# Two units' low halves taken by DMA at other places, one more unit split, and the order of a few steps around it

## The chip, the cores and the metric

The kernel runs on one core of a Trainium2 chip. The metric is the device time of one execution in microseconds (us); lower is better. The engines are named as the profile names them: PE (TensorE matmul), PEld (its weight loads), DVE (VectorE), ACT (ScalarE), POOL (GpSimd) and SP (SyncE), each with its own instruction queue; they meet only at semaphores.

## The reference

Two decoder layers on a tensor x of 256 tokens by 1024 channels, all in float32:

```python
def pool_conv_layer(x, ...):
    h = rms_norm(x, norm_g)
    a, bv, bg, z = split(h @ w_in)              # 1024 | 1024 | 1024 | 2048 columns
    ya = pool_w(trailing_mean(a) - a) * pool_scale      # windows of 2, 4, 8, 16 tokens
    u = causal_depthwise_conv(bv * sigmoid(bg), 31 taps) + conv_b
    yb = silu(layer_norm(u))
    return (concat(ya, yb) * silu(z)) @ w_out

def moba_layer(x, ...):
    q, k, v, z = split(rms_norm(x) @ w_in)      # 16 heads of 64
    q, k = per_head_rms_norm(q) * 64 ** -0.5, per_head_rms_norm(k)
    o = causal_softmax(q k^T - slope * distance) v
    return (o * silu(z)) @ w_out

x = x + pool_conv_layer(x); x = x + moba_layer(x)
```

With 256 tokens and attention blocks of 256 the second layer is plain causal attention over all tokens.

## The kernel before, in words

**Units.** All weights are cut into 49 units of 1 MB (128 partitions by 2048 floats), numbered in the order in which PE uses them: 0 to 7 gate and value of the convolution in turn (`BG`, `BV`), 8 to 11 the pooled channels (`A`), 12 to 15 the gates of the convolution half (`ZB`), 16 the pooling maps (`PW`), 17 to 20 the gates of the pooled half (`ZA`), 21 to 28 the output projection (`OA`, `OB`), 29 to 48 the second layer. SP loads unit n into place n % 4 of `raw`, once the last reader of unit n - 4 is through (L397).

**Native and split units.** A unit in `NATIVE` is multiplied as it is, in float32. Of any other, ACT writes a rounded copy `w_hi` in two halves of 1024 columns (`cut_hi`, L459), DVE writes `w_lo` = raw - `w_hi` (`cut_lo`, L723), and PE makes three products for each tile (`product`, L1058 to L1060). For the four units in `ADDED`, DVE has no part in this: ACT writes also -`w_hi` into `w_lo` (L462), and a DMA from POOL's queue adds raw to it (`added_low`, L424); PE waits for its landing. `cut_slot` says in which of four places of `w_hi` and `w_lo` a unit lies; ahead of unit 29 three of them rotate and the fourth holds unit 22 and then the convolution's result `yb`.

**The convolution.** In the loop over n = 1 to 21 (n names the unit that PE works on) ACT and DVE also make the 31 taps of eight channel tiles, two tiles a pair. `conv_plan` writes the order out before: with running sums of the free time of DVE and ACT in each unit (`slot_work` says what else they do there) it takes for each tap either a product by ACT (two multiplications, L542) that DVE adds (L845), or two fused multiply-adds on DVE (L841, called singles below). What is left at n = 21 goes to DVE as singles. Twelve products for each of two pairs are added by DMA instead: ACT multiplies (L518), POOL issues the adding DMA (L433), both by `side_items`. `window_sums` (L812 to L824) makes the pooling means of units 8 to 11 from `AP`, into which ACT copies a PSUM bank (L568) as soon as DVE is through with the copy before it.

**From the last tap to the output projection.** DVE adds the eight tiles to one (`fold_mean`, L858). PE takes the mean over channels by a matmul (`channel_mean`, L1181), DVE subtracts it (`centre`, L865), ACT squares (L467), DVE adds (L752), PE sums (L1135). `MEAN_AT` and `SUM2_AT` say behind which output product of units 21 to 24 PE makes these two matmuls: unit index in `OA`, row tile 0 or 1, column tile 0 to 7. Then come the root, `normalise`, the silu and `yb`, and behind them in the queues of ACT and DVE the cuts of units 26 to 28, which PE needs for `closing`.

**The second layer.** Units 33 to 44 run in three pairs for each octet of heads (keys, queries, values), 16 steps a pair, with scores, transposes and values of the octet before put between the steps. Keys and queries pass through PSUM bank `TR` for their transposes (L1251), and ACT copies them out (`qk_turn_out`, L680); the transposes of the probabilities (L1285) use the same bank. `KT_AT` gives the steps of the two key transposes, 28 and 32. `qk_squares` (L670) squares the banks of a pair, token tile by token tile.

## Time and profile before

| | |
|---|---|
| median of 3 runs | 332.69 us (332.54 to 332.81) |
| the profiled execution | 333.14 us |
| its span in the trace | 331.3 us |
| PE busy | 325.0 us (98%), 2212 matmuls |
| DVE busy | 256.2 us (77%) |
| ACT busy | 230.4 us (70%) |
| chain that ended last | PE 93%, DMA 3%, ACT 1%, DVE 1%, issue 1% |
| PE's clock | 0.9 or more of full speed in all 40 slices of the span, which is the level of 2.4 GHz |

An engine is read as waiting where a row carries "idle before", with what released it. The chain is followed back from the last instruction; a piece of it that isn't PE stands where PE waited, or just made it. A DMA issue on POOL is short, and its transfer lands long after; the time from issue to landing stands in an extra line of an answer on a tile or line. 331.3 us of span and 333.14 us of device time differ by 1.8 us that lie around the span.

### The profile page before, as it was taken

To read this page: it belongs to the slowest core of one execution; us is meant where nothing else is said; L and a number is where in the kernel's file an instruction comes from. 1 tells how busy PE (TensorE), PEld (TensorE's weight loads), DVE (VectorE), ACT (ScalarE), POOL (GpSimd) and SP (SyncE) were. 2 spreads that over 40 slices of the span, in tenths; PEclk is the share of its full clock that TensorE was granted. 3 is DMA by queue.
4 is the path that set the end of the run, shared out by engine and by line. 5 is a ranking of instruction groups with operands and counts; after the bars stand their busy time and mean duration, and the time that the engine had idled before them with its cause. 6 is when DMAs were issued, how large, how long until landed. Compare 5 with 4: busy or idle time off the path is not lost.

```text
span 331.3 us, 5760 instructions
## 1 busy us (share of the span) xinstructions
PE 325.0 (98%) x2212; PEld 296.2 (89%) x2212; DVE 256.2 (77%) x475; ACT 230.4 (70%) x429; POOL 51.8 (16%) x58
## 2 busy tenths in 40 slices
PE   8999999999999999999999999999999999999995
PEld 8899999999989999997999999988887776778885
DVE  2699989999689999996886898747556877748633
ACT  4677999994999897935775557824756666575630
POOL 0050024424422310120000000005500231400000
PEclk9999999999999999999999999999999999999999
DMA  7979488979999998676629343780634323200003
GB/s 277 409 272 357 146 267 217 202 164 349 276 252 345 167 380 296 130 174 208 254 103 403 130 133 133 279 347 10 245 127 166 135 99 132 108 0 2 2 0 127
DMA packets 12842, 64.77 MB, mean 195 GB/s; under 512 B 1424, under 2 KB 1552, under 8 KB 6544
## 3 DMA queue, kind: packets, MB, share of 16 engines
q1 hardware_dynamic: 8064, 53.78, 43.2%
q0 software_dynamic: 4608, 10.49, 17.3%
q8 instruction: 17, 0.28, 0.3%
q10 hardware_dynamic: 144, 0.15, 0.2%
q14 instruction: 9, 0.07, 0.1%
HBM read 52.88 MB, written 1.05 MB: 163 GB/s over the span
## 4 chain that ended last, share of the span: by engine, by line
PE 93%; DMA 3%; ACT 1%; DVE 1%; issue 1%; POOL 0%; ACTq 0%; POOLq 0%
PE bank L1058 25%; PE bank L1060 23%; PE bank L1059 23%; PE bank L1118 5%; PE bank L1092 4%; DMA w_lo<-raw 3%; PE bank L1166 2%; PE bank L1272 2%; PE bank L1299 2%; PE bank L1135 2%; PE bank L1126 2%; PE bank L1285 2%; PE bank L1251 1%; ACT scratch L467 1%; DVE scratch L752 1%
## 5 line engine op out<-in xcount | busy, mean ns | idle before, releaser
L723 DVE TENSOR_TENSOR w_lo<-raw,w_hi 128x1024 fp32r<-128x1024 f32 x76 | 90.3, 1222 | 19.6 <-ACT w_hi L459 19.4
L1058 PE MATMUL bank<-h_hi,w_hi 128*128 128x256 f32 x304 | 86.6, 285 | 0.4 <-DMA w_lo<-raw 0.4
L459 ACT CAST w_hi<-raw 128x1024 fp32r<-128x1024 f32 x84 | 84.4, 1048 | 2.7 <-PE bank L1060 2.7
L1060 PE MATMUL bank<-h_hi,w_lo 128*128 128x256 f32 x304 | 86.0, 283 | 0.0
L1059 PE MATMUL bank<-h_lo,w_hi 128*128 128x256 f32 x304 | 86.0, 283 | 0.0
L1058 PEld LDWEIGHTS bank<-h_hi,w_hi 128*128 128x128 f32 x304 | 58.3, 192 | 0.9 <-issue 0.8
L1059 PEld LDWEIGHTS bank<-h_lo,w_hi 128*128 128x128 f32 x304 | 58.3, 192 | 0.1
L1060 PEld LDWEIGHTS bank<-h_hi,w_lo 128*128 128x128 f32 x304 | 58.3, 192 | 0.0
L841 DVE SCALAR_TENSOR_TENSOR scratch<-scratch,params 128x256 f32<-128x256 f32 x108 | 44.1, 484 | 0.2
L1058 PE MATMUL bank<-w_hi,h_hi 128*128 128x512 f32 x96 | 39.2, 408 | 0.0
L1058 PE MATMUL bank<-ya_hi,w_hi 128*128 128x256 f32 x128 | 38.1, 297 | 0.0
L1060 PE MATMUL bank<-w_hi,h_lo 128*128 128x512 f32 x96 | 37.6, 391 | 0.0
L1059 PE MATMUL bank<-w_lo,h_hi 128*128 128x512 f32 x96 | 37.5, 391 | 0.0
L1060 PE MATMUL bank<-ya_hi,w_lo 128*128 128x256 f32 x128 | 36.1, 282 | 0.0
L1059 PE MATMUL bank<-ya_lo,w_hi 128*128 128x256 f32 x128 | 36.1, 282 | 0.0
L433 POOL DMA_DIRECT2D side_v<-side_ring x24 | 21.1, 908 | 70.8 <-ACT side_ring L518 65.7
L542 ACT ACTIVATE scratch<-scratch,params 128x256 f32<-128x256 f32 x76 | 31.9, 505 | 0.0
L845 DVE TENSOR_TENSOR scratch<-scratch 128x512 f32<-128x512 f32 x38 | 25.7, 692 | 1.4 <-ACT scratch L542 0.2
L1058 PEld LDWEIGHTS bank<-ya_hi,w_hi 128*128 128x128 f32 x128 | 24.4, 191 | 2.0 <-issue 1.7
L1059 PEld LDWEIGHTS bank<-ya_lo,w_hi 128*128 128x128 f32 x128 | 24.5, 191 | 0.1
L1060 PEld LDWEIGHTS bank<-ya_hi,w_lo 128*128 128x128 f32 x128 | 24.4, 191 | 0.0
L444 POOL TENSOR_SCALAR scratch<-scratch 128x8 f32<-128x8 f32 x8 | 4.3, 535 | 122.1 <-DVE scratch L1018 121.9
(106 smaller groups left out, 549.0 us busy)
## 6 DMA issues: line engine op xcount, KB each, us to landing
raw<-w SPq DMA_DIRECT2D x49, 1024.0 KB, 6.3
side_v<-side_ring POOLq DMA_DIRECT2D x24, 256.0 KB, 8.2
w_lo<-raw POOLq DMA_DIRECT2D x8, 512.0 KB, 8.1
X<-xT SPq DMA_DIRECT2D x2, 512.0 KB, 5.2
out<-X SPq DMA_DIRECT2D x4, 256.0 KB, 2.6
consts<-const SPq DMA_DIRECT2D x1, 290.0 KB, 13.5
params<-vec ACTq DMA_DIRECT2D x1, 149.0 KB, 4.9
```

The costliest lines, as they stand in the source:

```text
L433: pool.dma_start(side_v[:, pair, item % 2, :, :], side_home(pair, item), accum_op=ALU.add).then_inc(side_added[pair][item % 2], 16)
L459: nc.scalar.copy(halves(w_hi, cut_slot(n), half), halves(raw, n % RAW, half)).then_inc(hi_cut, 1)
L542: last = nc.scalar.mul(product_home(product)[:, i, :], U[:, c, k:k + S], column(CW + TAPS * c + k))
L723: nc.vector.tensor_tensor(halves(w_lo, cut_slot(n), half), halves(raw, n % RAW, half), halves(w_hi, cut_slot(n), half).bitcast(F32), ALU.s ...
L841: nc.vector.scalar_tensor_tensor(V[:, c, :], U[:, c, k:k + S], column(CW + TAPS * c + k), V[:, c, :], ALU.mult, ALU.add).then_inc(tap, 1)
L845: nc.vector.tensor_tensor(V[:, c:c + 2, :], V[:, c:c + 2, :], product_home(product), ALU.add).then_inc(tap, 1)
L1058: nc.tensor.matmul(dst, wh, ah, start=start, stop=False, skip_group_check=True)
L1059: nc.tensor.matmul(dst, wh, al, start=False, stop=False, skip_group_check=True)
L1060: return nc.tensor.matmul(dst, wl, ah, start=False, stop=stop, skip_group_check=True)
L1092: last = nc.tensor.matmul(dst, wr, (H if n else H0)[:, k, :], start=start, stop=stop, skip_group_check=True)
L1118: return nc.tensor.matmul(dst, wr, SZ[:, (KD if n in OB else 0) + tile, :], start=start and m % 2 == 0, stop=stop, skip_group_check=True)
L1126: nc.tensor.matmul(bank[7][:, 0:P], ones[:, :], ones[:, :], start=True, stop=True, skip_group_check=True)
```

## The change

`EARLY_ADDED` goes from (10, 14) to (9, 12), and unit 9 leaves `NATIVE`. So unit 9 is split and its low half is made by DMA, unit 12's too, and units 10 and 14 are cut by ACT and DVE. For the units up to 18 (`FOUR`) `cut_slot` rotates over all four places, and `slot_free(SPARE)` follows. In ACT's loop the cut of an early added unit stands ahead of the copy into `AP` and of the silu; in DVE's loop `window_sums` goes behind the taps at n = 10 (n + 2 = 12) alone. The two matmuls of the mean stand two column tiles later. `centre` goes behind the subtraction of `ya_lo`. In `qk_squares` of the queries the copies of the second key transpose stand between the two squares. `conv_plan` runs with the new sets and gives another order.

```diff
-NATIVE = frozenset((0, 9, 13, 16, 21, 23, 25))
-EARLY_ADDED = (10, 14)
+NATIVE = frozenset((0, 13, 16, 21, 23, 25))
+EARLY_ADDED = (9, 12)
 SPARE = 22
+FOUR, SLOT_ORDER = ZA[1], (3, 2, 0, 1)
...
-    return (cut_index(n) - (n > SPARE) - cut_index(Z1[0]) + 1) % 3
+    if n > FOUR:
+        return (cut_index(n) - (n > SPARE) - cut_index(Z1[0]) + 1) % 3
+    return SLOT_ORDER[(cut_index(FOUR) - cut_index(n)) % 4]
...
     if n == SPARE:
-        return released(PW)
+        return released(max(m for m in CUTS if m <= FOUR and cut_slot(m) == CUT - 1))
...
-MEAN_AT = 2, 0, 1
-SUM2_AT = 2, 1, 5
+MEAN_AT = 2, 0, 3
+SUM2_AT = 2, 1, 7
...
                 for pair, item in side_items(n):
                     side_product(pair, item)
+                if n + 3 in EARLY_ADDED:
+                    cut_hi(n + 3)
                 if n in A:
...
-                if n + 3 in EARLY_ADDED:
-                    cut_hi(n + 3)
...
                 for t in range(TT):
+                    if isq and t and KT_AT[1] == 32:
+                        qk_turn_out(octet, 0, 1)
...
-                            if s == KT_AT[half]:
+                            if s == KT_AT[half] != 32:
                                 qk_turn_out(octet, 0, half)
...
-                if m in A:
+                if m in A and n + 2 not in EARLY_ADDED:
                     window_sums(m - A[0])
...
                 taps(n)
+                if m in A and n + 2 in EARLY_ADDED:
+                    window_sums(m - A[0])
                 if n == OA[0]:
                     fold_mean()
-                    cut_lo(OA[2], (0,))
-                    centre()
-                    cut_lo(OA[2], (1,))
...
+            cut_lo(OA[2], (0,))
+            centre()
+            cut_lo(OA[2], (1,))
```

`cut_lo(OA[2])` is empty in both kernels, since unit 23 is native.

First place: ACT's queue from the copy of unit 8 into `AP` on (n = 8, 9, 10). Before, where L459 is a cast of half a unit, L542 a product for DVE, L518 a side product, L568 the copy into `AP`:

```order
L568 COPY scratch<-bank 128x2x256
L459 CAST w_hi<-raw 128x1024 x2
L542 ACTIVATE scratch<-scratch,params 128x256 x6
L518 ACTIVATE side_ring<-scratch,params 128x256 x4
L568 COPY scratch<-bank 128x2x256
L459 CAST w_hi<-raw 128x1024 x2
L542 ACTIVATE scratch<-scratch,params 128x256 x2
L518 ACTIVATE side_ring<-scratch,params 128x256 x4
```

Changed (the same lines, each 3 to 5 higher; L465 is the negated copy):

```order
L573 COPY scratch<-bank 128x2x256
L462 CAST w_hi<-raw 128x1024 x2
L521 ACTIVATE side_ring<-scratch,params 128x256 x4
L462 CAST w_hi<-raw 128x1024
L465 ACTIVATE w_lo<-w_hi 128x1024
L462 CAST w_hi<-raw 128x1024
L465 ACTIVATE w_lo<-w_hi 128x1024
L573 COPY scratch<-bank 128x2x256
L545 ACTIVATE scratch<-scratch,params 128x256 x2
```

The three products at n = 9 are gone; the cut of unit 12 with its negated copies stands ahead of the copy of unit 9 and of the next product.

Second place: DVE's queue from n = 20 to `centre`. Before, where L885 is the gating of `ya`, L845 the adding of a product, L841 a single, L858 `fold_mean`, L865 `centre`, L895 the low half of `ya`:

```order
L885 TENSOR_TENSOR scratch<-scratch 128x512
L845 TENSOR_TENSOR scratch<-scratch 128x512 x6
L885 TENSOR_TENSOR scratch<-scratch 128x512
L841 SCALAR_TENSOR_TENSOR scratch<-scratch,params 128x256 x14
L858 TENSOR_TENSOR scratch<-scratch 128x1024
L858 TENSOR_TENSOR scratch<-scratch 128x512
L858 TENSOR_TENSOR scratch<-scratch 128x256
L865 TENSOR_TENSOR scratch<-scratch,bank 128x512 x4
L895 TENSOR_TENSOR ya_lo<-scratch,ya_hi 128x512
```

Changed (each line 4 or 5 higher):

```order
L890 TENSOR_TENSOR scratch<-scratch 128x512
L850 TENSOR_TENSOR scratch<-scratch 128x512 x5
L846 SCALAR_TENSOR_TENSOR scratch<-scratch,params 128x256 x2
L890 TENSOR_TENSOR scratch<-scratch 128x512
L846 SCALAR_TENSOR_TENSOR scratch<-scratch,params 128x256 x24
L863 TENSOR_TENSOR scratch<-scratch 128x1024
L863 TENSOR_TENSOR scratch<-scratch 128x512
L863 TENSOR_TENSOR scratch<-scratch 128x256
L899 TENSOR_TENSOR ya_lo<-scratch,ya_hi 128x512
L870 TENSOR_TENSOR scratch<-scratch,bank 128x512 x4
```

Ten more singles stand at n = 21 (24 for 14), and the low half of `ya` has come ahead of `centre`.

Third place: ACT's queue at the end of the queries of the second octet. Before, where L670 squares a bank, L680 copies the transposed keys out, L637 and L632 belong to the octet before:

```order
L459 CAST w_hi<-raw 128x1024
L670 ACTIVATE scratch<-bank 128x512 x2
L680 ACTIVATE scratch<-bank,params 128x256 x2
L637 CAST ya_hi<-scratch 128x256
L459 CAST w_hi<-raw 128x1024
L632 COPY scratch<-bank 128x512
```

Changed (L675 squares, L685 copies out):

```order
L462 CAST w_hi<-raw 128x1024
L675 ACTIVATE scratch<-bank 128x512
L685 ACTIVATE scratch<-bank,params 128x256 x2
L675 ACTIVATE scratch<-bank 128x512
L640 CAST ya_hi<-scratch 128x256
L462 CAST w_hi<-raw 128x1024
```

The two copies stand between the squares.

## Rows read from the trace of the kernel before

**Rows 1.** PE's waits, whole span: who waited for whom, us, times, longest.

```profile
PE bank L1285 <- issue: 0.6, 1, 0.6
PE bank L1135 <- DVE scratch L752: 0.5, 1, 0.5
PE bank L1058 <- DMA w_lo<-raw: 0.4, 1, 0.4
```

**Rows 2.** Chain that ended last: start us, us, what; to the end of unit 9.

```profile
10.30 6.91 PE bank L1092 x32
63.28 6.91 PE bank L1092 x32
```

**Rows 3.** The same chain, the wait for unit 14.

```profile
84.66 9.99 DMA w_lo<-raw
94.78 0.36 PE bank L1058
```

**Rows 4.** The same chain, units 23 and 24.

```profile
149.12 0.87 PE bank L1118 x4
149.99 0.45 PE bank L1181 x2
...
156.11 0.70 PE bank L1135 x2
```

**Rows 5.** ACT in order of time: start, us, line, what, idle before.

```profile
52.29 3.30 ACT L518 ACTIVATE side_ring<-scratch,params 128x256 f32<-128x256 f32 x8
55.49 1.04 ACT L459 CAST w_hi<-raw 128x1024 fp32r<-128x1024 f32 x1
...
59.55 1.70 ACT L542 ACTIVATE scratch<-scratch,params 128x256 f32<-128x256 f32 x4
61.15 1.08 ACT L551 ACTIVATE scratch<-scratch,params 128x256 f32<-128x256 f32 x2
...
63.73 0.56 ACT L568 COPY scratch<-bank 128x512 f32<-128x512 f32 x1
64.20 2.00 ACT L459 CAST w_hi<-raw 128x1024 fp32r<-128x1024 f32 x2
```

**Rows 6.** DVE in order of time, 60 to 150 us.

```profile
65.49 2.35 DVE L723 TENSOR_TENSOR w_lo<-raw,w_hi 128x1024 fp32r<-128x1024 f32 x2
...
69.36 2.15 DVE L845 TENSOR_TENSOR scratch<-scratch 128x512 f32<-128x512 f32 x3
...
92.46 2.36 DVE L723 TENSOR_TENSOR w_lo<-raw,w_hi 128x1024 fp32r<-128x1024 f32 x2 [3.68 <-ACT w_hi L459]
...
135.19 4.68 DVE L845 TENSOR_TENSOR scratch<-scratch 128x512 f32<-128x512 f32 x6 [0.18 <-ACT scratch L542]
139.79 0.69 DVE L885 TENSOR_TENSOR scratch<-scratch 128x512 f32<-128x512 f32 x1
140.39 5.63 DVE L841 SCALAR_TENSOR_TENSOR scratch<-scratch,params 128x256 f32<-128x256 f32 x14
146.16 2.41 DVE L858 TENSOR_TENSOR scratch<-scratch 128x1024 f32<-128x1024 f32 x3
```

**Rows 7.** DVE, the cuts of units 26 to 28 ahead of `closing`.

```profile
168.86 6.90 DVE L723 TENSOR_TENSOR w_lo<-raw,w_hi 128x1024 fp32r<-128x1024 f32 x6 [0.25 <-ACT w_hi L459]
```

**Rows 8.** DMA queues in 57 to 63 us: packets, MB, share of 16 engines.

```profile
q0 software_dynamic: 575, 1.22, 112.3%
```

**Rows 9.** DMA queues in 73 to 87 us.

```profile
q1 hardware_dynamic: 518, 3.85, 68.3%
q0 software_dynamic: 509, 0.94, 36.4%
```

**Rows 10.** L424, all eight low halves added by DMA.

```profile
DMA to landing us min/median/max: 5.3/8.1/11.7
```

**Rows 11.** L433, the two side DMAs issued at 74.6 and 75.5 us.

```profile
DMA to landing us min/median/max: 12.1/13.2/14.2
```

**Rows 12.** ACT and PE around the second key transpose of the second octet.

```profile
278.58 0.60 PE L1251 MATMUL bank<-consts,scratch 128*128 128x128 f32 x4
...
280.48 0.60 ACT L670 ACTIVATE scratch<-bank 128x512 f32<-128x512 f32 x1 [1.46 <-DVE scratch L1018]
...
280.97 0.83 ACT L680 ACTIVATE scratch<-bank,params 128x256 f32<-128x256 f32 x2
...
281.90 0.85 PE L1285 MATMUL bank<-consts,scratch 128*128 128x128 f32 x6 [0.64 <-issue]
```

## The prediction

> **What bounds the kernel now.** I read PE's waits first: once it has begun, PE stood still for 0.6, 0.5 and 0.4 us in all [rows 1], and the page's chain is 93% PE. So the kernel is bound by PE's instruction stream, and an edit can win PE work or one of these waits, no more; or it can lose by a new wait. Then I read the chain in order of time for what a unit costs, and ACT's and DVE's timelines from 52 to 150 us for how close they run behind PE. They run close: between 92.46 and 146.02 us DVE works with one gap of 0.18 us [rows 6], and the sum behind the mean already waits for it (the 0.5 us on L1135) [rows 1]. What matters is when DVE reaches the end of `fold_mean`.
>
> **Unit 9 split.** A native unit takes 6.91 us; the eight split units from the end of unit 0 (17.21) to the start of unit 9 (63.28) take 46.07, so 5.76 each [rows 2]. PE gains 1.15 us. Unit 14 is no longer made by DMA, so the 0.4 us wait for its landing [rows 1, 3] goes too. Without new waits PE starts unit 12 at 63.28 + 3 x 5.76 = 80.56 and reaches the mean's matmul, now two column tiles later (4 recorded matmuls in 0.87) [rows 4], at 149.99 - 1.15 - 0.4 + 0.87 = 149.3 us.
>
> **What ACT has to do for it.** Until 53.9 us nothing differs (the first half of the side products at 52.29). A cut with negated copies lasts 59.55 - 55.49 = 4.06 us, a plain one 1.9, a side product or product 0.8, the first taps 1.0, the copy into `AP` 0.5 [rows 5]. In the new order: cut 9 to 58.0, two side products 59.6, cut 10 to 61.4, product and first taps 63.2, two side products 64.8, copy 65.3, cut 11 from 65.3 (before from 64.20), two side products 68.8, cut 12 with its negated copies 72.9, copy 73.4, product 74.2.
>
> **What DVE has to do.** It cuts units 10 and 14 now and neither 9 nor 12: before, three of these four were not its work, now two are not. That is one unit more, two times 1.13 = 2.3 us [rows 6]. The planner gives ACT fewer products: 33 for 38, and 118 singles for 108. A single is 5.63 / 14 = 0.40 us, an added product 0.6 to 0.72 [rows 6]. Up to unit 15 I follow it by sums. DVE comes to cut 11 at 65.2 and waits 1.1 for ACT; to the product at n = 10 at 71.8 and waits 2.4 (74.2 above); then 0.6 for the copy into `AP`, which in turn had to wait until `window_sums` were through, and 0.5 for cut 14. Its work between cut 11 and cut 15 was 92.46 - 3.68 - 65.49 = 23.3 us, now two singles more and two products fewer at the lower price each, 22.3. So it is at cut 15 at 65.2 + 22.3 + 4.6 = 92.1 us; the old gap of 3.68 us is used up and it stands 0.4 ahead of before. From there: ten singles more, +4.0; at n = 20 five products not held up by ACT (3.05) for six that took 4.87 at ACT's pace, -1.8; 0.5 at n = 14 for a first product; and at n = 19 a product now stands behind `ya_hi` in ACT's queue, which waits for DVE's own step: 0.5 + 0.8 us of wait, say 1.4 with the semaphores. Together -0.4 + 4.0 - 1.8 + 0.5 + 1.4 = +3.7. `fold_mean`, which ended at 148.57 [rows 6], ends at **152.2 us**, and PE has come for it at 149.3. PE's whole gain is gone there, and 1.4 us of slack besides.
>
> **Unit 12's low half.** Its first negated copy ends at 70.9, so the DMA is issued at 71.2 and 73.2 for the halves; PE wants them at 80.56 and 83.44. The software queue moved 1.22 MB in 6 us alone, 0.20 MB/us [rows 8], but 0.94 MB in 14 us, 0.067 MB/us, while the loads from SP moved 3.85 MB [rows 9]. In the changed kernel the loads of units 13, 14 and 15 start together at about 66 us, when unit 9's second half has landed, and at 0.275 MB/us their 3.1 MB last from 67 to 79 us. Ahead of unit 12 the queue holds four side products of 0.26 MB, of which 0.2 MB are through by 67; the other 0.82 MB take until 79.5; then the first half of 0.52 MB at 0.20 MB/us until 82.2, and 0.9 us to the semaphore: 83.1. That is 11.9 us behind its issue. Before, such landings took 9.99 for unit 14 [rows 3], 5.3 to 11.7 over all eight [rows 10] and 12.1 to 14.2 for side DMAs issued amid loads [rows 11]; I take 11.9, since it starts amid loads but ends behind them. PE stalls 2.5 us at unit 12. It gives back no more than its lead to DVE at first, but unit 16 ends 2.5 us later too, ACT's scaling of `YP` and its cut 19 stand behind that, and DVE needs cut 19: by the same sums 1.3 us of the 2.5 reach DVE. `fold_mean` then ends at **153.5**.
> The Trainium skill ("DMA: Bandwidth & Descriptors", the section on the anatomy of one DMA on the SWDGE path) fits such a DMA as 2.0 us and its bytes at 436 GB/s. That would be 3.2 us for a half, unit 12 in place by 77 us and no stall; the trace has 5.3 us as the shortest and disagrees, and the same page's section on SWDGE and HWDGE says that the two kinds share each engine in turn, which fits the 0.20 and 0.067 above. I keep the case without that stall as a rival.
>
> Unit 9's own halves are issued at 56.3 and 58.3, with no load on its way; two side DMAs lie ahead of them instead of the four ahead of unit 10's before. By the same 0.20 MB/us they land near 62 and 64.5 to 66.6 (wanted at 63.28 and 66.16), a stall of 0 to 0.5 us that unit 12's swallows. At 9.4 us, as far as the longest rows would go for the second, it would be 1.5, swallowed too.
>
> **From the mean to unit 27.** Mean and sum were 6.12 us apart by DVE and ACT's steps (149.99 to 156.11) [rows 4], while PE's own work between them is now 0.45 + 12 x 0.43 = 5.6: the chain of steps still decides. `ya_lo` ahead of `centre` overlaps with the mean's matmul but for 0.1 us. So the sum comes 153.5 - 149.95 = 3.6 us later than before, and with it `yb` and the cuts of 26 to 28, which ended at 175.76 [rows 7] when PE was about to begin `closing` at 176.1 (unit 26's end, two units and the native one behind the sum). That leaves 0.3 us of slack: +3.3 us there.
>
> **The key copies.** PE's pair of transposes waited 0.64 us at 281.3 [rows 12], and ACT's copies out of the same bank had ended at 281.7. ACT had been idle 1.46 us ahead of the second square, waiting for DVE. The transposes of the keys end at 279.2 [rows 12], so the copies (0.75) fit into that idle time and are done at 280.0; the square isn't delayed. This wait goes: **-0.6 us**. In the first octet the square may slip by a few tenths, with no attention step on PE to feel it. At worst this edit gives 0, if PE waits there for something else.
>
> **Places of the weight copies.** No cut before 176 us waited for a free place, and with four places each is free earlier: 0.
>
> **Sum.** +3.3 - 0.6 = +2.7 us on the profiled execution of 333.14: 335.8. The median of the runs lies 0.45 lower, so **335.4 us**, 0.8% slower.
>
> **Rivals.**
> (a) *DVE is late, but unit 12 isn't.* The adding DMAs get more than 0.067 MB/us and unit 12 lands within 9.4 us of issue. For it: 9.99 for unit 14 was as close to loads. Then `fold_mean` ends at 152.2: +1.4, so 334.1.
> (b) *The side that is faster.* DVE reaches the mean in time, by 149.3, since ACT's order costs it none of the waits I count (6.5 us in all) and the singles at the end fill old gaps. Then PE's stream decides: -1.15 - 0.4 - 0.6 = -2.2, so 330.5. The point from which it turns is a `fold_mean` ending before 150.8: above it the total grows. Against it: the waits follow from ACT's own sums, which have no gap between 52 and 75 us, and the extra work of DVE alone (2.3 + 4.0 less 3.5 for five products) is 2.8 us against 0.7 of slack.
> (c) *Unit 12 much later.* With 14.2 us from issue, PE stalls 4.8 and nearly all that is over 2 reaches DVE: `fold_mean` at 155.8, +5.0, so 337.7.
> (d) *Between.* DVE is 1 to 2 us less late than my sum and the gain in the second layer makes up for the rest: within 0.7 us of 332.7.
>
> **How the numbers follow.** Forecast 0.42, (a) 0.27, (b) 0.14, (d) 0.12, (c) 0.05. A measurement of this kernel can tell some 0.2%, 0.7 us, from no change. Slower by more: 0.42 + 0.27 + 0.05, less 0.02 for (a) at its low end, 0.72; within: 0.14; faster: 0.14. The range leaves out (b) and (c): 332.0 to 336.9.
>
> **What would show it.** After: unit 9 in 5.76 us; PE waits on L1058 for the low half at unit 12 (2.5 us, or 0 for (a)) and on L1181 or its weight load for `fold_mean`, which ends at 153.5 (152.2 for (a), under 149.3 for (b)); DVE waits 2.4 us ahead of the product at n = 10 and 1.4 at n = 19; no wait on the pair's transposes behind the keys'. The forecast falls if PE comes to the mean last, or if DVE is through its last single before 148 us.

## The result, and the profile of the changed kernel

| | before | changed |
|---|---|---|
| median of 6 runs | 332.75 us (332.54 to 332.84) | 342.26 us (340.37 to 343.72) |
| ratio, 95% interval | | 1.0275 (1.025 to 1.030) |
| the profiled execution | 333.14 us | 340.37 us |
| its span | 331.3 us | 338.0 us |
| mean granted clock of PE | 1.0 | 0.994; 0.984 to 0.990 in the other five runs |

The changed kernel is 9.5 us slower. The forecast was 2.7 us slower. Three parts make 9.5: the profiled executions differ by 7.2; before's profiled run lay 0.4 above its median; and the profiled run of the changed kernel was its fastest, 1.9 below its median.

PE's waits, whole span (who waited for whom, us in total, times, longest); they answer to [rows 1]:

```profile
PE bank L1065 <- DMA w_lo<-raw: 4.9, 1, 4.9
PE bank L1188 <- DVE scratch L863: 2.2, 1, 2.2
PE bank L1133 <- POOL eps L412: 1.0, 1, 1.0
PE bank L1065 <- DVE w_lo L728: 0.8, 1, 0.8
PE bank L1142 <- DVE scratch L757: 0.5, 1, 0.5
```

The 1.0 at the start is common to all kernels here. The 4.9 is unit 12's low half (L1065 is the old L1058), the 2.2 is the mean waiting for `fold_mean`, the 0.8 is `closing` waiting for the first cut of unit 26. The wait on the transposes of the probabilities, old L1285, is gone.

The chain that ended last (start, us, what), around unit 12; it answers to [rows 3]:

```profile
70.84 14.06 DMA w_lo<-raw
84.90 0.14 issue
85.04 0.55 PE bank L1065
85.59 0.21 PE bank L1066
85.80 0.21 PE bank L1067
...
88.44 0.12 PE bank L1066
88.56 0.12 PE bank L1067
```

The DMA was issued at 70.84 and landed 14.06 us later. Behind it a matmul of 256 columns takes 0.21 us in place of 0.12, until about 87.9: PE has its lower clock there. The windows (us, busy time of PE, PEld, DVE, ACT, POOL, then granted clock, DMA share, GB/s) say the same:

```profile
80.00:85.00 5.00, 0.17 (x2) 0.00 (x0) 4.65 (x9) 5.00 (x13) 2.18 (x3) 0.95 1.09 213
85.00:87.00 2.00, 1.96 (x9) 1.99 (x10) 1.59 (x3) 2.00 (x4) 0.43 (x1) 0.50 1.06 197
87.00:92.30 5.30, 5.30 (x42) 5.30 (x42) 4.69 (x8) 2.44 (x4) 1.72 (x2) 0.92 1.12 271
```

A clock of 0.50 is the level of 1.2 GHz. The mean of 0.95 in the first window puts its fall at 84.5 us, when PE had stood still for over 4 us, and the 0.92 in the third puts its return at about 87.9. Unit 12 therefore took from 85.04 to 92.28, 7.24 us, where its neighbours take 5.76.

DVE in order of time (start, us, line, what, idle before); it answers to [rows 6] and [rows 7]:

```profile
73.96 0.69 DVE L850 TENSOR_TENSOR scratch<-scratch 128x512 f32<-128x512 f32 x1 [2.44 <-ACT scratch L545]
...
85.63 2.36 DVE L728 TENSOR_TENSOR w_lo<-raw,w_hi 128x1024 fp32r<-128x1024 f32 x2 [0.41 <-ACT w_hi L462]
...
93.88 2.36 DVE L728 TENSOR_TENSOR w_lo<-raw,w_hi 128x1024 fp32r<-128x1024 f32 x2 [2.02 <-ACT w_hi L462]
...
121.65 2.36 DVE L728 TENSOR_TENSOR w_lo<-raw,w_hi 128x1024 fp32r<-128x1024 f32 x2 [1.73 <-ACT w_hi L462]
...
144.93 9.58 DVE L846 SCALAR_TENSOR_TENSOR scratch<-scratch,params 128x256 f32<-128x256 f32 x24
154.65 2.41 DVE L863 TENSOR_TENSOR scratch<-scratch 128x1024 f32<-128x1024 f32 x3
...
176.31 6.90 DVE L728 TENSOR_TENSOR w_lo<-raw,w_hi 128x1024 fp32r<-128x1024 f32 x6 [0.25 <-ACT w_hi L462]
```

The wait of 2.44 at n = 10 is the forecast 2.4. The two later ones are new: ACT was late with cut 15 (2.02) and with cut 19 (1.73). ACT's own rows say why:

```profile
92.32 0.60 ACT L579 ACTIVATE scratch<-bank 128x512 f32<-128x512 f32 x1 [2.87 <-PE bank L1067]
...
117.65 3.03 ACT L584 ACTIVATE scratch<-bank,params 128x256 f32<-128x256 f32 x8 [3.63 <-PE bank L1173]
```

The silu of unit 12's result stands ahead of cut 15 in ACT's queue and had to wait for PE's late unit 12; the scaling of `YP` waited for unit 16 in the same way, ahead of cut 19.

`fold_mean` ends at 157.06. The two traces have to be laid over each other at unit 0, which starts at 9.91 here and at 10.30 before [rows 2], a difference that arose before any edited step. On before's scale `fold_mean` ends at 157.45 (before 148.57, forecast 153.5), `closing` begins at 178.07 in place of 170.34, 7.7 later, and the key copies give 0.65 back. With the 0.4 of the earlier start, 7.7 - 0.65 - 0.4 = 6.7 us of span, which is what was measured. The other 0.5 of the 7.2 us between the two profiled executions lies around the span (2.4 us for 1.8).

Last, the DMA queues (packets, MB, share of 16 engines) in 66 to 79 us, and in 79 to 85 us; they answer to [rows 8] and [rows 9]:

```profile
q1 hardware_dynamic: 426, 3.14, 69.1%
q0 software_dynamic: 410, 0.74, 31.0%
...
q0 software_dynamic: 435, 1.27, 108.9%
```

Beside SP's loads the software queue moved 0.74 MB in 13 us, 0.057 MB/us; alone, 1.27 MB in 6 us, 0.21 MB/us. And POOL's issues, in which an idle time was spent waiting for ACT to be through with the source:

```profile
58.74 1.83 POOL L436 DMA_DIRECT2D side_v<-side_ring  x2
64.03 1.75 POOL L436 DMA_DIRECT2D side_v<-side_ring  x2 [3.45 <-ACT side_ring L521]
68.01 1.75 POOL L436 DMA_DIRECT2D side_v<-side_ring  x2 [2.23 <-ACT side_ring L521]
70.84 0.86 POOL L427 DMA_DIRECT2D w_lo<-raw  x1 [1.08 <-ACT w_lo L465]
```

The four side products of 64.03 to 68.9 landed at 76.1, 79.9, 81.1 and 82.5, then unit 12's halves at 84.9 and 87.4.

### The profile page after: what moved, and what is told of

Same layout as the page of the kernel before. It is cut to its first block, busy times and chain, and to the rows that moved or that the text cites. A ratio compares the mean times of both kernels' runs of the same rounds, so it can differ in the third digit from the quotient of the medians.

```text
span 338.0 us, 5786 instructions
## 1 busy us (share of the span) xinstructions
PE 324.9 (96%) x2228; PEld 296.9 (88%) x2228; DVE 258.8 (77%) x482; ACT 228.4 (68%) x421; POOL 51.3 (15%) x58
## 3 DMA queue, kind: packets, MB, share of 16 engines
HBM read 52.88 MB, written 1.05 MB: 160 GB/s over the span
## 4 chain that ended last, share of the span: by engine, by line
PE 68%; DVE 14%; ACT 9%; DMA 4%; issue 3%; POOL 0%; DVEq 0%; ACTq 0%; POOLq 0%
PE bank L1065 19%; PE bank L1067 17%; PE bank L1066 17%; DVE scratch L846 6%; DMA w_lo<-raw 4%; PE bank L1099 4%; ACT w_hi L462 3%; DVE w_lo L728 2%; PE bank L1279 2%; PE bank L1306 2%; DVE scratch L850 2%; ACT side_ring L521 2%; PE bank L1142 2%; PE bank L1133 2%; PE bank L1292 2%
## 5 line engine op out<-in xcount | busy, mean ns | idle before, releaser
L728 DVE TENSOR_TENSOR w_lo<-raw,w_hi 128x1024 fp32r<-128x1024 f32 x78 | 92.6, 1219 | 20.4 <-ACT w_hi L462 20.1
L1065 PE MATMUL bank<-h_hi,w_hi 128*128 128x256 f32 x320 | 91.8, 287 | 4.9 <-DMA w_lo<-raw 4.9
L1066 PE MATMUL bank<-h_lo,w_hi 128*128 128x256 f32 x320 | 91.1, 285 | 0.0
L1067 PE MATMUL bank<-h_hi,w_lo 128*128 128x256 f32 x320 | 91.1, 285 | 0.0
L1065 PEld LDWEIGHTS bank<-h_hi,w_hi 128*128 128x128 f32 x320 | 62.1, 194 | 5.1 <-ACT scratch L573 5.0
L1066 PEld LDWEIGHTS bank<-h_lo,w_hi 128*128 128x128 f32 x320 | 62.0, 194 | 0.1
L1067 PEld LDWEIGHTS bank<-h_hi,w_lo 128*128 128x128 f32 x320 | 62.0, 194 | 0.0
L846 DVE SCALAR_TENSOR_TENSOR scratch<-scratch,params 128x256 f32<-128x256 f32 x118 | 48.1, 476 | 0.2
L1065 PE MATMUL bank<-w_hi,h_hi 128*128 128x512 f32 x96 | 39.2, 408 | 0.0
L1065 PE MATMUL bank<-ya_hi,w_hi 128*128 128x256 f32 x128 | 38.1, 297 | 0.0
L436 POOL DMA_DIRECT2D side_v<-side_ring x24 | 21.2, 904 | 76.1 <-ACT side_ring L521 61.4
L545 ACT ACTIVATE scratch<-scratch,params 128x256 f32<-128x256 f32 x66 | 27.9, 507 | 0.0
L1065 PEld LDWEIGHTS bank<-ya_hi,w_hi 128*128 128x128 f32 x128 | 24.4, 191 | 2.0 <-issue 1.7
L850 DVE TENSOR_TENSOR scratch<-scratch 128x512 f32<-128x512 f32 x33 | 21.7, 686 | 5.9 <-ACT scratch L545 5.4
```

Of the source, the lines that this page charges most:

```text
L436: pool.dma_start(side_v[:, pair, item % 2, :, :], side_home(pair, item), accum_op=ALU.add).then_inc(side_added[pair][item % 2], 16)
L545: last = nc.scalar.mul(product_home(product)[:, i, :], U[:, c, k:k + S], column(CW + TAPS * c + k))
L728: nc.vector.tensor_tensor(halves(w_lo, cut_slot(n), half), halves(raw, n % RAW, half), halves(w_hi, cut_slot(n), half).bitcast(F32), ALU.s ...
L846: nc.vector.scalar_tensor_tensor(V[:, c, :], U[:, c, k:k + S], column(CW + TAPS * c + k), V[:, c, :], ALU.mult, ALU.add).then_inc(tap, 1)
L850: nc.vector.tensor_tensor(V[:, c:c + 2, :], V[:, c:c + 2, :], product_home(product), ALU.add).then_inc(tap, 1)
L1065: nc.tensor.matmul(dst, wh, ah, start=start, stop=False, skip_group_check=True)
```

## The experiments

Twelve kernels, and before run beside them (medians 332.58 to 332.76). First what the change is made of, then unit 12's wait, then the mean. The last two columns are of the profiled execution. e7, e9, e11 and e12 leave out a part of the computation.

| run | built on | median us | ratio to before | span | PE at 1.2 GHz after a wait at |
|---|---|---|---|---|---|
| e1_keys | before | 331.93 | 0.9978 (0.9969 to 0.9987) | 330.0 | none |
| e5_before_plus | before | 331.29 | 0.9954 (0.9942 to 0.9967) | 329.7 | none |
| e10_ten_twelve | before | 337.66 | 1.0148 (1.013 to 1.0166) | 335.3 | unit 12 |
| e4_nine_fourteen | changed | 333.89 | 1.0038 (1.0024 to 1.0053) | 331.7 | none |
| e2_hold | changed | 341.20 | 1.0244 (1.0213 to 1.0274) | 336.9 | the mean |
| e6_pool_first | changed | 337.99 | 1.017 (1.014 to 1.0201) | 335.6 | unit 12 |
| e3_filler | changed | 340.09 | 1.0232 (1.0211 to 1.0253) | 338.2 | the mean |
| e8_filler_twice | changed | 338.92 | 1.0195 (1.0179 to 1.021) | 337.0 | none |
| e7_no_wait12 | changed | 336.61 | 1.0114 (1.0095 to 1.0134) | 334.7 | the mean |
| e11_nowait_filler | e7 | 335.13 | 1.0072 (1.0057 to 1.0087) | 333.6 | none |
| e9_fewer_singles | e4 | 332.24 | 0.9986 (0.9973 to 1.0) | 330.1 | none |
| e12_mean_back | e9 | 330.73 | 0.9942 (0.9925 to 0.9958) | 329.7 | none |

### e1: the key copies alone

```diff
                 for t in range(TT):
+                    if isq and t and KT_AT[1] == 32:
+                        qk_turn_out(octet, 0, 1)
...
-                            if s == KT_AT[half]:
+                            if s == KT_AT[half] != 32:
```

> The kernel before with one part of the change alone: the copies of the second key transpose stand between the two squares of the queries. Theory: PE's wait of 0.64 us ahead of the pair's transposes was for these copies, so it goes and the time is 332.75 - 0.6 = 332.1 us. Rival: PE waited there for the probabilities or the bank behind, and the time stays at 332.7.

331.93 us (331.69 to 332.22), 0.7 us below before (332.60 beside it). ACT, and then PE, at the place of [rows 12]:

```profile
278.69 0.84 ACT L682 ACTIVATE scratch<-bank,params 128x256 f32<-128x256 f32 x2 [0.19 <-PE bank L1253]
279.95 0.60 ACT L672 ACTIVATE scratch<-bank 128x512 f32<-128x512 f32 x1 [0.42 <-DVE scratch L1020]
...
280.58 0.82 PE L1287 MATMUL bank<-consts,scratch 128*128 128x128 f32 x6
```

The copies lie in what was ACT's idle time, and PE's transposes have no idle time before them. This part of the change does what was forecast.

### e10: one number changed in the kernel before

```diff
-EARLY_ADDED = (10, 14)
+EARLY_ADDED = (10, 12)
```

> The kernel before with one number changed: low halves of units 10 and 12 by DMA instead of 10 and 14; unit 9 stays native, and the rest is as it was. My theory: it is the place of unit 12 amid the loads of units 13 to 15 that costs, whatever is split: its halves land 12 us or more behind their issue, PE stalls 2 us or more at unit 12, a stretch at half clock of about 3.4 us follows, and the time is 337 to 341. Rival: with the older order of the steps and DVE less loaded the stall is absorbed, or the halves land in 10 us since unit 9's second half doesn't hold back SP's loads: then 332 to 334.

337.66 us, 4.9 above before, with unit 9 still native and all other steps in the old order. PE's wait:

```profile
PE bank L1058 <- DMA w_lo<-raw: 3.2, 1, 3.2
```

And its windows:

```profile
80.00:84.00 4.00, 1.46 (x13) 1.25 (x11) 3.83 (x9) 3.58 (x8) 1.75 (x2) 1.00 1.03 310
84.00:88.00 4.00, 3.37 (x17) 3.40 (x18) 3.96 (x5) 3.98 (x7) 0.00 (x0) 0.62 1.07 221
```

The low half landed 11.6 us behind its issue (I had expected 12 or more), PE stood still for 3.2 and then ran at the lower clock for most of 4 us. So unit 12's place alone costs about half of the change's loss; splitting unit 9 isn't needed for it. SP issued the loads of units 13 to 15 from 70.0 us on here and from 64.1 on in the changed kernel, where unit 9's place in `raw` is free once its DMA has landed and not once PE has read it.

### e4: unit 14 in place of unit 12, in the changed kernel

```diff
-EARLY_ADDED = (9, 12)
+EARLY_ADDED = (9, 14)
```

> The changed kernel with unit 14 made by DMA and unit 12 cut by ACT and DVE, as before the change; unit 9 stays split with its low half by DMA, and the planner runs with this set. Theory (unit 12's place amid the loads of 13 to 15 is the cause): a wait of under 2 us at unit 14, DVE still late for the mean by 1 to 3 us, 333 to 336 us. Rival (making unit 9 by DMA is itself what delays the engines): still above 338 us.

333.89 us: 8.4 of the 9.5 us are gone with one number (from which `conv_plan` also writes another order). PE's clock is full throughout, unit 14's halves land 6.6 and 8.5 us behind their issue, and PE waits for them 0.3. What is left is PE's wait at the mean:

```profile
PE bank L1188 <- DVE scratch L863: 1.7, 1, 1.7
```

and on DVE, at the end of the 24 singles:

```profile
148.35 2.41 DVE L863 TENSOR_TENSOR scratch<-scratch 128x1024 f32<-128x1024 f32 x3
```

`fold_mean` ends at 150.76 and PE has come for it 1.7 earlier. e9 and e12 below take this up.

### e2: hold back the load of unit 14

```diff
+                    if n == 14:
+                        for half in range(2):
+                            sp.wait_ge(lo_added[ADDED.index(12)][half], 16)
```

> The changed kernel, but SP holds back the load of unit 14 (and with it the ones behind) until both low halves of unit 12 have landed. Theory 1 (the loads of units 13 to 15 slow the adding DMAs of unit 12 down, that landing stalls PE 4.9 us, and the slower clock behind it costs another 1.5): the halves land within 9 us of issue, no wait at unit 12, no stretch at half clock; what is left over is the late DVE, 334 us. Theory 2 (the POOL queue's own backlog of side products is what delays it): the landing stays at 12 us or more behind the issue and the time above 338. Theory 3 (all the loss comes from unit 12): 330.5 us.

341.20 us, which none of the three theories had. Unit 12 lands 9.4 and 9.9 us behind its issue, and PE waits 0.2 for it in place of 4.9. SP has the load of unit 13 alone under way there and not three: 1.04 MB in 66 to 79 us in place of 3.14, and the software queue moves 1.75 MB in place of 0.74. But the load of unit 14 now starts at 82.58, and ACT and DVE come to its cut too late (rows in order of time):

```profile
87.57 1.99 ACT L465 CAST w_hi<-raw 128x1024 fp32r<-128x1024 f32 x2 [3.13 <-DMA raw<-w]
...
88.65 2.36 DVE L731 TENSOR_TENSOR w_lo<-raw,w_hi 128x1024 fp32r<-128x1024 f32 x2 [3.65 <-ACT w_hi L465]
```

PE's waits then have:

```profile
PE bank L1191 <- DVE scratch L866: 6.6, 1, 6.6
```

The whole wait has moved to the mean, in one piece, with a stretch at the lower clock behind it. This shows the contention, and also that curing unit 12's stall doesn't help while DVE loses the same time elsewhere.

### e6: unit 12 ahead of two side products in POOL's queue

```diff
+                if n == 9:
+                    added_low(12)
...
-                if n + 3 in EARLY_ADDED:
+                if n + 3 in EARLY_ADDED and n != 9:
```

> The changed kernel with the two adding DMAs of unit 12 issued by POOL ahead of the two side products of n = 9, instead of behind them; the side products then wait for ACT's negated copies, and land later. Theory (the software queue is served in order, at 0.057 MB/us while SP's loads run and 0.20 without them, so what stands ahead of the halves counts): 0.52 MB less ahead, the first half lands 2.6 us or more earlier, 81.5 to 82.5 us instead of 84.9, the wait at unit 12 falls to 1.5 to 2.5 us, the time to about 338. Rival (the order in the queue does not matter, only when they are issued): landing at 84 to 85 and 342.

337.99 us. The halves land 11.7 and 12.2 us behind their issue in place of 14.1 and 14.5, 2.3 us less for two side DMAs fewer ahead of them (0.52 MB; at the 0.21 MB/us that the queue has in those last microseconds, 2.5). PE's wait falls to 2.5, which is the stall of my forecast, and `fold_mean` ends at 154.71 with unit 0 starting at 9.70. On before's scale that is 155.3, where my sum for a stall of 2.5 had 153.5; here a slow stretch follows the stall, from 82.4 to 85.8 us, which my sum didn't have.

### e3 and e8: matmuls of ones where PE would stand still

e3 puts 20 of them ahead of unit 12; e8 also puts 10 ahead of the mean.

```diff
+                if n == 12:
+                    for _ in range(20):
+                        nc.tensor.matmul(bank[7][:, 0:P], ones[:, :], ones[:, :], start=True, stop=True, skip_group_check=True)
...
+                            for _ in range(10):
+                                nc.tensor.matmul(bank[3][:, 0:P], ones[:, :], ones[:, :], start=True, stop=True, skip_group_check=True)
```

> The changed kernel with 20 float32 matmuls on the constant tile ones, 128 columns each, some 4.4 us of work, ahead of unit 12, where PE stands idle 4.9 us. The output is untouched. Theory: the idle time at unit 12 is followed by a stretch at 1.2 GHz which costs 1.5 us in the profiled run and more in others (mean clock 0.984); kept busy, PE stays at 2.4 GHz, unit 12 takes 5.76 us and not 7.24, and the time is about 339 us with little spread. Rival: the clock has no share in the loss, and the time stays at 342.3.

> The changed kernel with the filler of 20 matmuls on ones ahead of unit 12 and 10 more (2.2 us) ahead of the mean's matmul, where PE waits 2.2 us too. Theory: with the first filler alone PE fell to 1.2 GHz behind the second wait; with both it stays at 2.4 GHz throughout, and the time is 338.5 to 339.5 us with a spread below 1 us. Rival: the clock falls whatever PE does there, and the time stays at 340 with a spread of 2 us.

e3 340.09, e8 338.92 us. In both, unit 12's data lands as late as in the changed kernel (14.51 us behind its issue in e3), but PE waits only 0.7 and 0.8 for it and goes on at full clock. The chain of e3 around unit 12:

```profile
71.07 14.51 DMA w_lo<-raw
85.58 0.04 issue
85.62 0.38 PE bank L1065
86.00 0.12 PE bank L1066
86.12 0.12 PE bank L1067
```

In e3 a wait of 2.2 us at the mean was then followed by a stretch of 3.4 us at 1.2 GHz, from 157.0 on (0.62 is the mean of 156 to 160 us), which is why e3 missed the 339 us and the little spread that I expected (339.42 to 341.54). In e8, with matmuls there too, the clock is full until PE's work ends, and the time is the expected one, with a spread of 1.1 us. The window of e3:

```profile
156.00:160.00 4.00, 3.44 (x9) 2.82 (x10) 3.50 (x6) 1.84 (x4) 0.00 (x0) 0.62 0.46 142
```

and of e8:

```profile
156.00:160.00 4.00, 4.00 (x21) 3.46 (x20) 3.19 (x6) 2.26 (x4) 0.00 (x0) 1.00 0.35 104
```

From the changed kernel to e8 the median falls by 3.3 us, the profiled execution by 1.5 (340.37 to 338.82). The profiled run of the changed kernel had one stretch at 1.2 GHz, 3.4 us long or 1.7 us of full clock lost. DVE's first cut for `closing` tells what it cost: it begins at 176.31 with unit 0 at 9.91 in the changed kernel, and at 175.36 with unit 0 at 9.81 in e8, so 166.40 and 165.55 us behind unit 0. One stretch cost 0.85 us of the time here. Four of the changed kernel's other five runs have a mean clock of 0.984 or 0.985 over 340 to 341 us, which is 5.3 lost, as in three such stretches, and they took longest, 342.20 to 343.72; the two with 0.994 and 0.990 took 340.37 and 340.49. Where the further stretches lie can't be said, since only one run has a trace.

### e7 and e11: no wait at unit 12

e7 multiplies `w_hi` where unit 12's `w_lo` would stand; e11 is e7 with 17 matmuls of ones ahead of the mean.

```diff
+                elif n == 12:
+                    pe.wait_ge(hi_cut, 2 * cut_index(n) + half + 1)
...
-                return raw[:, n % RAW, a:b], (w_hi[:, s, a:b], w_lo[:, s, a:b])
+                return raw[:, n % RAW, a:b], (w_hi[:, s, a:b], (w_hi if n == 12 else w_lo)[:, s, a:b])
```

and in e11 besides, ahead of the mean's matmul:

```diff
+                            for _ in range(17):
+                                nc.tensor.matmul(bank[3][:, 0:P], ones[:, :], ones[:, :], start=True, stop=True, skip_group_check=True)
```

> The changed kernel in which PE takes unit 12's rounded copy in the place of its low half and waits for ACT's casts instead of the DMA: that part of the computation is left out, the number and size of the matmuls is the same, and all DMAs and the order on ACT and DVE stay. It measures what is left of the loss without the stall at unit 12. Theory (the forecast's own sum without the stall): fold_mean ends at 152.2 us, PE waits for it 2 to 3 us, 334.1 us in all. Rival 1 (all of the loss is the stall): 330.5. Rival 2 (ACT and DVE are late on their own account by more than the sums say): 336 or more.

> The changed kernel without a wait for unit 12's low half (PE multiplies w_hi in its place, so unit 12's product is incomplete) and with 17 more matmuls of ones (3.7 us of PE) ahead of the mean's matmul, where PE would otherwise stand still for 3.8 us. If the half clock behind that wait costs what I read from the records (3.4 us at half speed), the time falls from 336.6 to about 334.9 (334.1 to 335.3), and the granted clock stays full throughout. If the clock behind the wait costs nothing, since DVE and ACT's steps decide there anyway until closing, the time stays at 336.6.

e7 336.61, e11 335.13 us. Without a stall at unit 12 `fold_mean` is late all the same. PE's largest wait in e7:

```profile
PE bank L1190 <- DVE scratch L863: 3.8, 1, 3.8
```

and DVE's rows:

```profile
140.79 9.58 DVE L846 SCALAR_TENSOR_TENSOR scratch<-scratch,params 128x256 f32<-128x256 f32 x24
150.50 2.41 DVE L863 TENSOR_TENSOR scratch<-scratch 128x1024 f32<-128x1024 f32 x3
```

It ends at 152.91 with unit 0 at 10.51, so at 152.7 on before's scale, where the forecast had 152.2. The 24 singles start at 140.6 on that scale, against 145.3 in the changed kernel: 4.75 us of PE's stall and slow unit 12 reach DVE. PE came to the mean at 149.1 (forecast 149.3), stood still for 3.8, and lost another 1.5 us to the clock behind that: with matmuls in the gap (e11) the median is that much lower and the clock full. The traces show 0.9 of it (the medians of the spans, 334.4 and 333.3, differ by 1.1): from the end of `fold_mean` to DVE's first cut for `closing` it takes 20.18 us in e7 (152.91 to 173.09) and 19.25 in e11 (152.70 to 171.95). So e7's 336.61 is not my theory's 334.1 but the second rival's "336 or more", and not for its reason: DVE was 0.5 us later than the sums say, and the clock is most of the rest.

### e9 and e12: what the split of unit 9 is worth

e9 is e4 without taps 26 to 30 of one pair, ten singles less at n = 21. e12 puts the mean and the sum back where they were.

```diff
-    left = {pair: [k for k in range(1, TAPS) if k not in side_taps(pair)] for pair in range(4)}
+    left = {pair: [k for k in range(1, TAPS) if k not in side_taps(pair) and not (pair == 2 and k > 25)] for pair in range(4)}
```

```diff
-MEAN_AT = 2, 0, 3
-SUM2_AT = 2, 1, 7
+MEAN_AT = 2, 0, 1
+SUM2_AT = 2, 1, 5
```

> The kernel with low halves of units 9 and 14 by DMA, and ten single taps fewer (taps 26 to 30 of the third pair of channel tiles are left out, so this part of the convolution isn't computed): DVE has 14 singles instead of 24 behind n = 20, all else as it is. My theory is that in the version with 9 and 14 only DVE's tail eats the gain of splitting unit 9: then fold_mean ends some 4 us earlier than 150.8, PE's wait at the mean (1.7 us) goes, the wait for the cuts ahead of closing (0.8 us) shrinks, and the time falls from 333.9 to about 331 (330.4 to 331.8), below the 331.9 of the kernel before with the key copies moved. Rival: the split doesn't pay 1.15 us on PE, or something other than DVE's last taps holds the mean; then the time stays at 333 or more.

> The kernel of e9_fewer_singles (low halves of 9 and 14 by DMA, taps 26 to 30 of the third pair of channel tiles left out) with the two matmuls of the mean back at their places in the kernel before, two column tiles earlier. In e9 PE came to the mean at 149.6 us, only 0.4 earlier than before, and stood 0.8 us ahead of closing; from the sum to closing's first low half the steps take 14.1 us, PE's own work 13.4 with the late places and 14.2 with the early ones. My theory: the two column tiles, not DVE, gave back the rest of unit 9's gain. Then PE comes to the mean at 148.7 us (fold_mean ends at 147.2, so no wait), the wait of 0.8 ahead of closing goes, and the span falls by 0.8 to 329.3, the time from 332.2 to 331.4 (330.9 to 331.8). Rival: the places don't matter, since the steps from the mean to closing take as long wherever they start; then 332.2 stays.

e9 332.24 us: the wait at the mean is gone and 1.65 us with it, but I had expected 331 and the miss has a cause. In its waits 0.8 is left ahead of `closing`; e12 hasn't got it and takes 330.73, 1.5 lower, where I had expected 331.4 (330.9 to 331.8). PE in order of time in e9 (what lies between left out):

```profile
155.71 0.70 PE L1142 MATMUL bank<-scratch,ones 128*128 128x256 f32 x2 [0.50 <-DVE scratch L757]
...
162.00 7.07 PE L1125 MATMUL bank<-scratch,raw 128*128 128x256 f32 x32
169.84 0.36 PE L1065 MATMUL bank<-w_hi 128*128 128x256 f32 x1 [0.77 <-DVE w_lo L728]
```

The chain of e12, which is PE all the way here:

```profile
155.25 0.70 PE bank L1142 x2
155.95 0.86 PE bank L1125 x4
...
162.57 6.91 PE bank L1125 x32
169.47 0.26 PE bank L1065
```

From the sum to unit 26 the steps of DVE and ACT take 14.1 us. PE's own work there is 14.2 in e12 (155.25 to 169.47) and in before (156.11 to 170.33), and two column tiles less, 13.35, in e9 and the changed kernel (e9: 155.71 to 169.07, where PE begins to wait). So with the late places PE comes 0.8 too early, and the mean itself 0.87 later: each column tile by which the mean is moved later takes its 0.43 us out of the gain. The span of e12 was 329.7 where I had expected 329.3: this run waited 1.1 for unit 14's landing (e9's 0.6), and it is the slowest of its four. So the places explain 0.8 of the 1.5 us; the medians of the spans, 330.1 and 329.0, differ by 1.1, and what is above 0.8 isn't traced.

### e5: the parts that pay, without those that cost

The key copies of e1, the mean one column tile earlier than before, and the cut of an added unit ahead of the copy into `AP`; low halves of 10 and 14, unit 9 native.

```diff
-MEAN_AT = 2, 0, 1
+MEAN_AT = 2, 0, 0
...
+                if n + 3 in EARLY_ADDED:
+                    cut_hi(n + 3)
                 if n in A:
...
-                if n + 3 in EARLY_ADDED:
-                    cut_hi(n + 3)
```

> The kernel before with the key copies between the squares, the mean's matmul one column tile earlier (2, 0, 0), and the cut of units 10 and 14 ahead of the copy into AP and the silu, all other things as before the change. Expected: the 0.64 us of the key copies goes (measured alone: -0.7); the mean comes 0.43 us earlier, so the sum's wait of 0.5 us shrinks to about 0.1; unit 14's low half is issued up to 2.9 us earlier and its wait of 0.4 us goes. Together 331.0 to 331.3 us. Rival: the earlier cut 14 delays the last copy into AP by 1.7 us, DVE's later work with it, and the mean loses what is won: 332 us or more.

331.29 us (330.85 to 331.50), 0.46% below before and the fastest version here that computes the whole reference. The sum's wait of 0.5 [rows 1] is gone. Unit 14's DMA is issued 2.1 us earlier (82.55 for 84.66) but lands at 94.3, 11.7 us behind its issue where before it was 9.99. With the two traces laid over each other at unit 0 (9.98 here) it is issued 1.8 us earlier and lands 0.1 earlier, and PE still waits 0.4 for it, against what I expected. An earlier issue only joined the queue earlier. The key copies and the sum's wait make 1.15 of the 1.5 us that the median fell by; the rest isn't traced, so that the time met its range is in part luck.

## Why the prediction was wrong

The direction was right and so was the place: unit 12's landing, then DVE late for the mean. The size was off by a factor of 3.5: 9.5 us for 2.7. Point by point:

**Unit 9 split, unit 14's wait.** Right. Unit 12 could have started at 80.5 on before's scale (forecast 80.56), 11 units at 5.76 behind unit 0. Unit 9's halves landed 5.4 and 6.1 us behind their issue, no stall. Without unit 12's, PE came to the mean at 149.1 (e7), forecast 149.3.

**ACT's order and DVE's waits.** Right: on before's scale cut 11 began at 65.3 and the product at n = 10 was done at 74.2, both as forecast; DVE's wait 2.44 for 2.4, the copy's 0.71 for 0.6, cut 14's 0.41 for 0.5. `fold_mean` without the stall: 152.7 (e7) for 152.2.

**Unit 12's landing: the first step that failed.** It was issued when I had said (70.84, which is 71.2 on before's scale), and landed 14.1 us later where I had 11.9, at 85.3 on that scale for 83.1. I put four side products ahead of it, 0.2 MB of them through by 67 us, and 0.067 MB/us until 79.5. But two more, issued at 58.7 and 59.6, lay behind unit 9's halves; they landed at 65.3 and 67.2, so none of the four had landed by 67. SP's loads began at 64.1 (64.5 on before's scale), when unit 9's second half landed; I had 66. In 66 to 69 us the software queue moved 0.02 MB, and over 66 to 79 its rate was 0.057. So about 0.33 of the four's 1.05 MB was left at 79 us, against almost none in my sum; at 0.21 MB/us it and the half of 0.52 MB last until 83.1, or 83.5 on before's scale, 1.3 us later than my 82.2. The other 0.9 is the end: the half landed 1.8 us behind this count, where I had put 0.9 to the semaphore. By then some 0.4 MB of what stands behind it in the queue had moved too (1.27 MB in all in 79 to 85), so the queue doesn't finish one transfer before the next; more than that isn't traced. My rows for rival (c) had the landing, 12.1 to 14.2 us for transfers issued amid loads [rows 11]; I gave it 0.05 because I let the queue be empty too early. Its time, 337.7, would still have been 4.6 too low: its `fold_mean` ended at 155.8, 1.65 too early, and it had no term for the clock.
The Trainium skill ("DMA: Bandwidth & Descriptors", SWDGE vs HWDGE vs iDMA) says that each DMA engine takes turns between the two kinds of queue; 0.057 MB/us beside the loads and 0.21 alone agree with sharing, though not in equal parts, and so does e2, where two loads fewer brought the landing down to 9.4. The Trainium skill's fit (same page, Anatomy of one DMA), 2.0 us and the bytes at 436 GB/s, gives an estimate of 3.2 us for a half; the traces disagree, every landing of such a half was between 4.8 and 15.7 us.

**The clock: not in the prediction at all, and the largest miss.** I priced a wait of PE at its own length and the clock behind it at nothing. In the profiled run it lay at 1.2 GHz for 3.4 us, of which PE was at work for 2.85, so unit 12 took 1.5 us more, and 0.85 of that reached the time; in most other runs the mean clock is lower still. By e8 against the changed kernel the clock is 3.3 us of the median.

**What passes to DVE: the second step that failed.** I let 1.3 of 2.5 us through, by way of cut 19 alone, and said that unit 12's stall would only give back PE's lead at first. But cut 15 stands in ACT's queue behind the silu that reads unit 12's bank; DVE began it at 94.3 on before's scale where I had 92.1, and e7, without the stall, has 92.2. The products behind it lost 0.7 more, and cut 19 came on top. Of the 6.4 us that PE lost at unit 12 (4.9 and 1.5) 4.75 reached the singles. e6 says the same at a smaller size: with a stall of 2.5 and its slow stretch `fold_mean` ended at 155.3, not 153.5.

**From the mean to `closing`.** Right: sum +7.8, `closing` +7.7 on one scale (the slack is 0.1, not 0.3). But this made rival (b) too low: I took 330.5 for the case in which DVE is in time, without the 0.87 by which the mean stands later. e9 is that case and takes 332.2; only with the places moved back, e12, is it 330.7. With DVE in time the split of unit 9 wins nothing over the key copies alone (331.93) at the late places, and 1.2 at the early ones.

**Key copies.** -0.6 forecast, -0.65 in the trace, -0.7 in the median of e1.

**The places of the weight copies.** Counted at nothing. No wait in the trace is put down to them, but no run took this part out alone. Nor did one take out the new order of ACT's cuts and copies or of `window_sums`; their share of the waits is read from the traces alone.

**The account.** Three medians divide the 9.5 us. Before to e11, no late landing and no slow clock: 332.75 to 335.13, +2.4, DVE's lateness at the mean less the key copies. e11 to e8, the late landing without the clock: 338.92, +3.8. e8 to the changed kernel, the clock: 342.26, +3.3. In my sum the same three were +1.4 (rival (a), 334.1), +1.3 and 0. The misses of 1.0, 2.5 and 3.3 add up to the 6.9 us between 335.4 and 342.26. Of the 1.0, `fold_mean` being 0.5 later and the slack being 0.2 smaller are seen in the traces; the other 0.3 isn't traced. As a case without the stall, rival (a) needed the clock as well: e7 took 336.61, 1.5 above e11.

## What to carry to other kernels

Price a DMA by its place in the queue: write down every transfer issued ahead of it with its bytes, also those that lie ahead of the ones ahead, and move them at the rate measured beside loads until the loads end. Price a wait of PE at its length and at what a slow stretch behind it may cost (0.85 and 0.9 us for one of 3.4 us in the two pairs of traces here, and there can be several), and follow it into the queues of the engines that read PE's results: what stands behind such a reader is late too. And a matmul that is moved later to wait less takes its own delay out of the gain, and PE's work out from under the steps that follow.

## What the runs showed of the chip

A DMA that adds 0.5 MB took 4.8 to 15.7 us from issue to landing over these kernels. Holding back two loads brought unit 12's from 14.1 to 9.4 (e2), and two side products fewer ahead of it to 11.7 (e6).

In the profiled runs PE's clock fell to 1.2 GHz around single waits of 6.6, 4.9, 3.8, 3.2, 2.5 and, in e3, 2.2 us, and came back some 3.4 us after it fell (6.8 in e2, behind the 6.6). Waits of 1.7 us and less show none, and the waits of 2.2 at the mean in the changed kernel and in e6 neither.

The changed kernel's runs also spread more, 340.37 to 343.72 us, where before's lie in 332.54 to 332.84 and e8's, at full clock, in 338.81 to 339.92. That isn't so of every kernel here: e10's, with a slow stretch, lie in 337.11 to 338.24, and e9's, at full clock, in 331.32 to 333.10.
